# Two transformer blocks on one core: the gathered tokens of four experts ahead of the other twelve

## What is computed

```python
h = modulate(rms_norm(x, norm2_g[l]), sh2, sc2)
x = x + g2[:, None, :] * expert_choice_ffn(h, w_router[l], w_gate_e[l], w_up_e[l], w_down_e[l])
if need_ctx:                              # layer 0 only
    xc = xc + cg1[:, None, :] * yc
    hc = modulate(rms_norm(xc, norm2_g[l]), csh2, csc2)
    xc = xc + cg2[:, None, :] * expert_choice_ffn(hc, w_router[l], w_gate_e[l], w_up_e[l], w_down_e[l])
```

## Time and profile before

| | us |
|---|---|
| median of three runs | 2353.37 (2352.24 to 2354.55) |
| the profiled execution | 2359.08 |
| its span, from the first to the last instruction | 2357.3 |
| TensorE busy in it | 2051.3 (87%) |
| VectorE busy | 681.4 (29%) |
| ScalarE busy | 415.8 (18%) |
| weights and other data moved | 598.14 MB |

### The profile page before, as it was taken

How to read it: one execution, slowest core, us unless ns; L and a number is a source line. 1 busy time by engine, 2 the same in 40 slices (tenths; PEclk the granted TensorE clock), 3 DMA queues, 4 the chain that set the end, 5 groups by cost and what they waited for, 6 DMA issues and landing times.

```text
span 2357.3 us, 21451 instructions
## 1 busy us (share of the span) xinstructions
PE 2051.3 (87%) x8566; PEld 1011.5 (43%) x8566; DVE 681.4 (29%) x1619; ACT 415.8 (18%) x864; POOL 0.2 (0%) x4
## 2 busy tenths in 40 slices
PE   6989899998888988898899967788776678979998
PEld 3445444444433333333554433343221246748863
DVE  2266210135211212123551142122211148740001
ACT  3045200012200000002151012103100032540000
POOL 0000000000000000000000000000000000000000
PEclk8999899999999999999999978999898888989999
DMA  9129722311499999996285537999999962122432
GB/s 363 72 82 361 263 83 61 116 72 72 198 429 429 429 429 426 429 428 253 96 310 164 199 147 313 419 403 426 429 428 429 430 248 93 51 92 95 166 139 80
DMA packets 111613, 598.14 MB, mean 254 GB/s; under 512 B 9255, under 2 KB 15223, under 8 KB 86811
## 3 DMA queue, kind: packets, MB, share of 16 engines
q1 hardware_dynamic: 107920, 591.82, 62.5%
q10 hardware_dynamic: 3595, 4.95, 0.6%
HBM read 595.71 MB, written 1.05 MB: 253 GB/s over the span
## 4 chain that ended last, share of the span: by engine, by line
PE 70%; DMA 20%; DVE 6%; ACT 2%; issue 2%; DVEq 0%; SPq 0%; ACTq 0%
PE bank L1271 23%; DMA weight_ring<-in_w_up_e 13%; PE bank L1637 10%; PE bank L623 6%; PE bank L1664 4%; PE bank L1620 4%; PE bank L1220 3%; PE bank L642 3%; DMA arena<-in_w_up_e 3%; PE bank L1237 3%; DMA weight_ring<-in_w_down_e 2%; PE bank L1477 2%; PE bank L424 2%; PE bank L1426 2%; DMA weight_ring<-in_w_ada 2%
## 5 line engine op out<-in xcount | busy, mean ns | idle before, releaser
L1271 PE MATMUL bank<-weight_ring,arena 128*128 128x512 f32 (+1 forms) x1328 | 559.8, 584 | 4.4 <-DVE small L2201 1.8
L1271 PEld LDWEIGHTS bank<-weight_ring,arena 128*128 128x128 f32 x1328 | 252.3, 190 | 307.7 <-issue 298.1
L1637 PE MATMUL bank<-weight_ring,arena 128*64 128x512 f32 x832 | 252.3, 645 | 42.2 <-DMA weight_ring<-in_w_up_e 26.1
L1620 PE MATMUL bank<-weight_ring,arena 128*32 128x512 f32 x848 | 160.5, 787 | 82.2 <-DMA weight_ring<-in_w_up_e 62.7
L1664 PE MATMUL bank<-weight_ring,arena 128*64 128x512 f32 (+1 forms) x800 | 180.7, 598 | 11.9 <-DMA weight_ring<-in_w_down_e 7.8
L1220 PE MATMUL bank<-const,arena 128*128 128x128 f32 (+4 forms) x812 | 119.9, 300 | 58.1 <-DVE arena L2102 10.2
L623 PE MATMUL bank<-arena,weight_ring 128*128 128x256 f32 x704 | 152.2, 379 | 0.9 <-DVE small L2249 0.9
L1220 PEld LDWEIGHTS bank<-const,arena 128*128 128x128 f32 (+4 forms) x812 | 104.6, 176 | 111.8 <-issue 69.5
L2976 ACT ACTIVATE arena<-bank 64x512 f32<-64x512 f32 (+1 forms) x64 | 37.7, 590 | 648.5 <-PE bank L1637 410.6
L1637 PEld LDWEIGHTS bank<-weight_ring,arena 128*64 128x64 f32 x832 | 80.4, 148 | 165.3 <-issue 157.2
L623 PEld LDWEIGHTS bank<-arena,weight_ring 128*128 128x128 f32 x704 | 133.7, 190 | 19.3 <-issue 1.1
(11 more groups left out here) (383 smaller groups left out, 1819.0 us busy)
## 6 DMA issues: line engine op xcount, KB each, us to landing
weight_ring<-in_w_up_e SPq DMA_DIRECT2D x53, 2048.0 KB, 14.0
weight_ring<-in_w_gate_e SPq DMA_DIRECT2D x52, 2048.0 KB, 16.3
weight_ring<-in_w_down_e SPq DMA_DIRECT2D x50, 2048.0 KB, 14.2
weight_ring<-in_w_in SPq DMA_DIRECT2D x25, 2048.0 KB, 10.2
weight_ring<-in_w_ada SPq DMA_DIRECT2D x24, 2048.0 KB, 12.6
arena<-in_w_down_e SPq DMA_DIRECT2D x14, 2048.0 KB, 14.2
arena<-in_w_gate_e SPq DMA_DIRECT2D x12, 2048.0 KB, 15.7
weight_ring<-in_w_mod SPq DMA_DIRECT2D x12, 2048.0 KB, 9.5
```

Of the source, the lines that this page charges most:

```text
L1271: mm = pe.matmul(b[:, 0:c1 - c0], lhs[:, k, t * P:t * P + P], slot_view(r)[:, k, c0:c1], start=(k == 0), stop=(k == ks - 1))
L1620: mm = pe.matmul(b[c:c + R, :], xgT[1][:, KH * half + k, e, :], wide(r)[:, k, n * 512:n * 512 + 512], start=(half == 0 and k == 0), stop=( ...
L1637: mm = pe.matmul(banks_[n][c:c + R, :], xgT[l][:, KH * half + k, e, 0:R], wide(r)[:, k, n * 512:n * 512 + 512], start=(half == 0 and k == ...
```

## The change

The gather is divided by experts. `EARLY` is 128: the columns of experts 0 to 3. First, the early columns of all eight k are gathered (16 matmuls of 128 columns for each stream, two or four values of k in one bank, evicted in pieces of 128 columns); then both halves of expert 0's gate and up run; then the picks are turned, and the other 384 columns (experts 4 to 15) are gathered for both streams through pool A, evicted by ScalarE alone (`take_gathered`). Before `gate_up(4, 0)` TensorE waits for these evictions. In layer 0 the fifth slot joins at take 8 instead of 6, and is free when the last late gather is done. VectorE weighs the picks after its early evictions.

```diff
+EARLY = 4 * CAP
...
-            def gather(l, s, k, b, pool):
+            def gather(l, s, k, dst, c0=0, c1=E * CAP):
 
                 for t in (2 * s, 2 * s + 1):
-                    mm = pe.matmul(b[:, :], xn2[:, t, every8(k)], pick[l][:, t, :], start=(t == 2 * s), stop=(t == 2 * s + 1))
-                mm.then_inc(S("full" + pool), 1)
+                    mm = pe.matmul(dst, xn2[:, t, every8(k)], pick[l][:, t, c0:c1], start=(t == 2 * s), stop=(t == 2 * s + 1))
+                return mm
...
                 if l == 0:
                     pe.wait_ge(S("pick_ready"), due("pick_ready"))
-                gather_first(range(0, 2))
+                    for k0 in range(0, KD, 4):
+                        b = bank("A")
+                        for j in range(4):
+                            mm = gather(0, 0, k0 + j, b[:, j * EARLY:j * EARLY + EARLY], 0, EARLY)
+                        mm.then_inc(S("fullA"), 1)
                 turn_tokens(last)
-                gather_first(range(2, 4))
                 logits(l, last, bank("D"))
-                gather_first(range(4, 5))
                 turn_logits(last)
-                gather_first(range(5, 8))
                 turn_aff(last, bank("D"))
...
-                for k in range(5):
-                    pool = "DA"[k % 2]
-                    gather(l, last, k, bank(pool), pool)
...
+                early_jobs = []
+                for k0 in range(0, KD, 4):
+                    for pool, at in (("D", k0), ("A", k0 + 2)):
+                        b = bank(pool)
+                        for j in range(2):
+                            mm = gather(l, last, at + j, b[:, j * EARLY:j * EARLY + EARLY], 0, EARLY)
+                        mm.then_inc(S("full" + pool), 1)
+                    early_jobs.append((T.n["freeD"], T.n["freeA"]))
...
                 pair = next_pair(0)
-                slots.add(RING, 4 if l else 6)
-                pe.wait_ge(S("freeD"), POOL + low_dve)
-                pe.wait_ge(S("freeA"), POOL + low_act)
+                slots.add(RING, 4 if l else 8)
+                wait_early(0)
                 gate_up(0, 0, pair)
-                for k in range(5, KD):
-                    gather(l, last, k, late if k == 6 else bank("A"), "DA"[k % 2])
-                high_act = T.n["freeA"]
+                wait_early(1)
+                gate_up(0, 1, pair)
                 turn_picks(l, last, "A")
-                put_copied = T.n["freeA"]
+                for s in range(ns):
+                    for k in range(KD):
+                        b = bank("A")
+                        gather(l, s, k, b[:, 0:E * CAP - EARLY], EARLY, E * CAP).then_inc(S("fullA"), 1)
+                gathered = T.n["freeA"]
                 if l == 0:
-                    extra_free[0, RING] = ("fullA", put_copied)
-                pe.wait_ge(S("freeD"), POOL + late_job)
-                pe.wait_ge(S("freeA"), POOL + high_act)
-                gate_up(0, 1, pair)
+                    extra_free[0, RING] = ("fullA", gathered)
                 for e in range(E):
                     turned = next_bank()
                     if e + 1 < E:
                         pair = next_pair(e + 1)
+                        if e + 1 == EARLY // CAP:
+                            pe.wait_ge(S("freeA"), POOL + gathered)
                         gate_up(e + 1, 0, pair)
```

On ScalarE the evictions of the late columns stand ahead of the silu of expert 0:

```diff
-                take_gathered(l, last, range(1, KD, 2))
+                take_early(l, last, 2, 2)
                 take_picks(last)
+                for s in range(ns):
+                    take_gathered(l, s)
```

More of the change, by code:

```diff
@@ L1566, in experts @@
                 last = ns - 1
-                def gather_first(ks):
-                    if l == 0:
-                        for k in ks:
-                            gather(0, 0, k, bank("A"), "A")
                 if l == 0:
                     pe.wait_ge(S("pick_ready"), due("pick_ready"))
-                gather_first(range(0, 2))
+                    for k0 in range(0, KD, 4):
[3 more added lines that the diff above has]
+                        mm.then_inc(S("fullA"), 1)
                 turn_tokens(last)
-                gather_first(range(2, 4))
                 logits(l, last, bank("D"))
-                gather_first(range(4, 5))
                 turn_logits(last)
-                gather_first(range(5, 8))
                 turn_aff(last, bank("D"))
@@ L1806, in experts @@
                         gate_up(e + 1, 1, pair)
-                    if e == 4:
-                        pe.wait_ge(S("freeA"), POOL + put_copied)
                     if e % 4 == 0 and e:
@@ L2361, in experts @@
                 take_places(l, last)
-                for k in range(0, KD, 2):
-                    if k == 6:
-                        weigh_picks(l, last)
+                for k0 in range(0, KD, 4):
                     dve.wait_ge(S("fullD"), due("fullD"))
                     b = bank_of("D", T.n["fullD"])
-                    dve.tensor_scalar(xgT[l][:, k, :, CAP * last:CAP * last + CAP], b[:, :].rearrange("p (e c) -> p e c", c=CAP),
-                                      mod_cols[:, 2 * l + 1, 0, k, last:last + 1], mod_cols[:, 2 * l + 1, 1, k, last:last + 1], ALU.mult, ALU.add).then_inc(S("freeD"), 1)
-                    dve.wait_ge(S("freeD"), due("freeD"))
+                    for j in range(2):
+                        k = k0 + j
+                        signal = "freeD" if j else "dve_step"
+                        dve.tensor_scalar(xgT[l][:, k, 0:EARLY // CAP, CAP * last:CAP * last + CAP],
+                                          b[:, j * EARLY:j * EARLY + EARLY].rearrange("p (e c) -> p e c", c=CAP),
+                                          mod_cols[:, 2 * l + 1, 0, k, last:last + 1], mod_cols[:, 2 * l + 1, 1, k, last:last + 1], ALU.mult, ALU.add).then_inc(S(signal), 1)
+                        dve.wait_ge(S(signal), due(signal))
+                weigh_picks(l, last)
                 R = CAP * ns
@@ L2833, in exponentiate_logits, with take_columns, take_gathered, take_early @@
                 act.wait_ge(S("aff_exp_ready"), due("aff_exp_ready"))
-            def take_gathered(l, s, ks):
-                for k in ks:
+            def take_columns(l, s, k, src, e0, e1, signal):
+                act.activation(xgT[l][:, k, e0:e1, CAP * s:CAP * s + CAP], src.rearrange("p (e c) -> p e c", c=CAP),
+                               ACT.Identity, scale=mod_cols[:, 2 * l + 1, 0, k, s:s + 1], bias=mod_cols[:, 2 * l + 1, 1, k, s:s + 1]).then_inc(S(signal), 1)
+                act.wait_ge(S(signal), due(signal))
+            def take_gathered(l, s):
+                for k in range(KD):
                     act.wait_ge(S("fullA"), due("fullA"))
                     b = bank_of("A", T.n["fullA"])
-                    act.activation(xgT[l][:, k, :, CAP * s:CAP * s + CAP], b[:, :].rearrange("p (e c) -> p e c", c=CAP),
-                                   ACT.Identity, scale=mod_cols[:, 2 * l + 1, 0, k, s:s + 1], bias=mod_cols[:, 2 * l + 1, 1, k, s:s + 1]).then_inc(S("freeA"), 1)
-                    act.wait_ge(S("freeA"), due("freeA"))
+                    take_columns(l, s, k, b[:, 0:E * CAP - EARLY], EARLY // CAP, E, "freeA")
+            def take_early(l, s, first, n):
+                for k0 in range(first, KD, 4):
+                    act.wait_ge(S("fullA"), due("fullA"))
+                    b = bank_of("A", T.n["fullA"])
+                    for j in range(n):
+                        take_columns(l, s, k0 + j, b[:, j * EARLY:j * EARLY + EARLY], 0, EARLY // CAP, "freeA" if j == n - 1 else "act_step")
             def experts(l):
@@ L2852, in experts @@
                     root_tile(3)
-                    take_gathered(l, 0, range(0, 2))
+                    take_early(l, 0, 0, 4)
                 modulate_tokens(l, last)
-                if l == 0:
-                    take_gathered(l, 0, range(2, 5))
                 exponentiate_logits(last)
-                if l == 0:
-                    take_gathered(l, 0, range(5, 8))
                 for s in range(ns):
```

9 lines of the change are left out of this document (3 added, 6 removed).

## The result

Over 20 executions each, the changed kernel takes **2359.06 us** at the median (2355.35 to 2364.96) and the kernel before 2353.24. The medians differ by 5.8 us. The ratio of the alternating runs is 1.0032, which is 7.5 us, with a 95% interval of 1.0023 to 1.0040: 5.4 to 9.4 us slower. The forecast was 2363, 0.4% slower. The profiled execution of the changed kernel has a span of 2355.6 us, which is *shorter* than the 2357.3 of before. That has to be resolved first, and a common mark does it: the moment at which SyncE issues take 2 of layer 0. Nothing that the change touches lies ahead of it.

A forecast was written before the change was run, and what follows sets the result against it. The prediction took each expert stage to be bound by a gapless stream of 2 MB weight transfers, started by freed ring slots. Layer 0's +12.8 and layer 1's -3.0 gave +9.8 us on 2353.37: 2363 us, range 2356.5 to 2368.

The forecast's parts named there:

- faster: Rival: the weight stream has slack and catches up, so only earlier first releases count, -4.1 and -3.0 us, 2346.3; chance 0.05.
- Early record, 0.254 us: Each 128-column early gather record costs 0.254 us with its stepped load, so 32 records take 8.1 us.
- Quick load: Rival: stepped loads only have longer latency, an early record takes 0.129 us at full clock; +3.9 us, 2357.3; chance 0.17.
- no overlap: Rival: load and stream take turns in early gathers, 0.425 us a record; +16.9 us, 2380; chance 0.03.
- Picks of layer 0, 1.4 us earlier: Layer 0's router: stream 1's picks are ready at 599.95 us instead of 601.35.
- Both halves, 14.0 us: Layer 0, after the early gathers: gate_up(0,0) and gate_up(0,1) run at once, 7.02 us each.
- cold-clock rival: Rival: gate_up(0,0) starts at 1.2 GHz and takes 1.8 us more in each layer, 2366.8; chance 0.15.
- Late gathers, 20.7 us: Layer 0, ahead of gate_up(1,0): 64 records of 384 columns for both streams, 0.324 us each, 20.7 us.
- The wait over silu, 4.3 us: Layer 0: after the late gathers, gate_up(1,0) waits 4.3 us for a bank, over silu and multiplication; before 3.4.
- Layer 0 in all, +12.8: Layer 0's expert stage: take 9 goes out 12.8 us later, and nothing makes it good.
- Layer 1, -3.0: Layer 1: early gathers take 8.1 us instead of 11.07, first release 3.0 us earlier, no gap in the stream.
- The sum, +9.8: Whole kernel: layer 0's +12.8 and layer 1's -3.0 us give +9.8 us, everything outside the expert stages unchanged.

The follow-up runs named there:

- e0: The kernel before, profiled once more without an edit; one execution, 2355.39 us.
- e2: The change in layer 1 alone, layer 0 as in the kernel before; median 2349.95 us, ratio 0.9975 to the kernel before.
- e8: Changed kernel, layer 0: stream 0 gathered whole, own silu area, three late k ahead of gate_up(1,0), fifth slot at take 10; 2346.47 us, 0.9964 to before.
- e1: The change in layer 0 alone, layer 1 as in the kernel before; median 2368.74 us, ratio 1.0051 to the kernel before.
- e5: Changed kernel with early gathers loading 128 neighbouring token columns instead of every eighth; ratio 1.0028 to the kernel before.
- e3: Changed kernel with stream 0 of layer 0 gathered whole in its old spread places; median 2352.20 us, ratio 0.9990 to the kernel before.
- e6: Changed kernel, layer 0 gathering stream 1's late columns before stream 0's, with expert 0's silu between; ratio 1.0026 to the kernel before.
- e4: Kernel before with only the fifth slot of layer 0 joining at take 8 instead of 6; ratio 1.0022 to the kernel before.
- e6b: The same kernel as e6, run again without an edit; ratio 1.0025 to the kernel before.

## Why the prediction was right

**What bounds the kernel:** held. The stream shifts as a whole. Counted from the first release, the last take of layer 0 follows 442.9 to 443.1 us later in before, e0 and e2, and 442.7 us later in e8, the kernels without a hole there; in layer 1, 454.8 to 456.3 us later in all kernels but one, and 459.1 in the profile of before. The rival *faster* (the stream catches up) falls with the window from 660 us, share 1.01 and 428 GB/s as before, and with e1.

**Early record, 0.254 us:** measured 7.92 us for 32 in both layers, 0.248 us each (by the group, 0.245). Quick load (0.129) and no overlap (0.425) both fall. The working held too: at full clock e5 has 0.117 us for the dense record, where it had taken 0.129, and 0.122 for the step, where it had taken 0.125. e5 also comes near what the quick-load rival had reckoned: its picks in layer 0 come 1.1 us earlier than in the changed kernel, as written there, and its early records of layer 1 take 5.85 us (5.8). The rule of the Trainium skill ("TensorE: Matmul & The Clock Gate", LDWEIGHTS) goes by the number of columns alone, so by it the two kernels would have been equal here. The trace disagrees: 7.65 us against 3.73 for the same 32 records, and 325 ns a load against 286 on average in e5, where half the loads of that line are dense.

**Picks of layer 0, 1.4 us earlier:** this step failed. The early gathers of stream 1 began 595.94 - 567.76 = 28.18 us after the mark instead of 601.35 - 572.91 = 28.44, 0.3 us earlier. The chain above shows why: the logits took 1.97 us and two small turns 0.70 and 0.60, against these rows of the chain of before:

```profile
584.14 1.00 PE bank L1452 x16
...
587.18 0.22 PE bank L1220 x2
...
592.67 0.23 PE bank L1220 x2
```

and, as windows, before and then after:

```profile
584.00:591.00 7.00, 7.00 (x32) 4.80 (x32) 1.70 (x8) 3.85 (x5) 0.00 (x0) 1.00 0.01 5
```
```profile
580.25:587.50 7.25, 3.22 (x22) 1.13 (x22) 1.70 (x8) 1.51 (x2) 0.00 (x0) 0.50 0.00 0
```

The granted clock was 0.50 there, 1.00 before. TensorE was busy 7.00 of 7 us before, and 3.22 of 7.25 after: the gathers that I counted as removed from the path had kept the clock up for the small steps between them. e3 and e8 show it, which put these gathers back and have 1.00, 0.22 and 0.23 us again. The kernel before had the warning in its own layer 1, where no gathers stand between these steps: its chain has 1.97, 0.70 and 0.60 us there (from 1397.53), at a granted clock of 0.50. Those slower steps cost 0.97 + 0.48 + 0.37 us = 1.8 us; the working had priced them at full clock (the logits also began 12.5 us after the mark instead of the 12.9 that I had reckoned, which gives some back). Takes 4 and 5 came 3.2 us earlier instead of 4.1.

**Both halves, 14.0 us:** 13.88; turned picks 1.02 (1.0). The cold-clock rival falls: no 1.8 us on top. The clock was at half when the early gathers began (0.50 until 600 us), but that cost them next to nothing, since a stepped record takes the same at either level, and it was at full before gate_up(0,0) started at 603.86.

**Late gathers, 20.7 us:** 20.78, and e3 shows that each of them counts. **The wait over silu, 4.3 us:** 643.32 - 639.54 = 3.8. **Gate_up(1,0) at 8.8:** 8.79, and e6 shows that wait and clock belong together: without the one, 7.02.

**Layer 0 in all, +12.8:** take 9 came 84.37 - 71.22 = 13.15 us later: 1.1 us of the gain at the picks did not come, and the wait, the early gathers and the two halves were 0.8 us shorter between them. Another 0.3 us arise before the last take (+13.5). The idle stretches were predicted at 9.1 and 8.1 us; in the trace the transfers paused for 8.4 and 7.0. With the start 3.2 us earlier and the end 13.5 us later, 16.7 us had to be lost; 1.3 of them were not found in these two.

**Layer 1, -3.0:** first release 3.2 us earlier, no gap; the last take 4.1 us earlier than in e0, e1 and e4. Counted from the first release that is within the 1.5 us by which kernels differ. In the two shown profiles it looks like 7.1, of which 3 are chance.

**The sum, +9.8, against +7.5 by the ratio (5.4 to 9.4) and +5.8 at the medians:** the layers give +13.4 - 4.1 = +9.3; the rest of the span, the second block, gives -2.8, in code that nobody changed. The largest difference of clock is between 80 and 100 us after the last take, before and then after:

```profile
1967.03:1987.03 20.00, 19.05 (x78) 12.17 (x79) 14.66 (x35) 7.36 (x14) 0.00 (x0) 0.74 0.25 93
```
```profile
1968.28:1988.28 20.00, 18.86 (x81) 12.17 (x82) 16.17 (x37) 7.54 (x14) 0.00 (x0) 0.83 0.24 93
```

Kernels with both layers changed had it at 467.3 to 467.8 in six of seven profiles, the others at 469.8 to 470.3 in all five; e6b had 471.3 with the same instructions as e6. So I put it down to the clock (over the whole rest 0.95 in the changed kernel and 0.94 before) and not to the work of the block, which is the same; what decides it is not shown. As said at e2, it came only where both layers were changed. The prediction had taken everything outside the expert stages as fixed; that term accounts for 2.8 of the 4 us between 2363 and 2359. The forecast of a profiled span of about 2367 missed by 11.5 us (2355.6): besides these 2.8 us, the mark fell 5.1 us earlier and layer 1 had been 3 us long in the profile of before, both by chance, and layer 1 gained 1 us more than forecast, layer 0 lost 0.7 more.

## What to carry to other kernels

Where a stage is a stream of transfers, write down for every slot which instruction frees it, and take the transfers in flight between two releases as the budget: work put between them beyond it is paid in full, and so is work ahead of the first release. Dividing a step helps only if its second part is fed in between releases in pieces that fit (e8), not in one block ahead of the next release. And compare traces from a common mark, stretch by stretch: the span alone had the wrong sign here.

## What the runs showed of the hardware that I had not expected

- Taking filler matmuls out of a chain of small steps halves TensorE's clock for those steps: 16 logit records took 1.97 us instead of 1.00, at 0.50 instead of 1.00, and 1.00 us again with the matmuls back in place (e3). Work that waits in the gaps isn't free to remove.
- Early records of 128 columns whose weights are loaded from columns eight apart took 0.239 us each at full clock, against 0.117 with dense ones, and those of 256 columns 0.244: the load sets the pace there. At half clock the two were some 0.24 and 0.22. Halving the clock costs such records hardly anything, and loading them densely gains little behind a wait.
- Stretches of unchanged code outside the streams took 326.4, 329.5 or 332.4 us, and the same again in the two kernels that were profiled twice (326.4 and 326.4 for the kernel before; 332.4 and 332.5 for e6), with a granted clock of 1.00 or 0.92 over the same 64 records; the three profiles with 332.3 to 332.5 are just those whose last take of layer 0 falls 496.8 to 496.9 us after the mark. An edit of 6 us in one stage can be taken back by this in another. Which feature of the timing sets it stays open; no run varied it alone.
